# Squares of q and k ahead of weight splits and of the last scans, a softplus one split later, and unit-matrix products on TensorE around two norms

## What is computed

```python
xr, yr, qkv, z, beta_raw, alpha_raw = split(h @ w_in)          # layer 0, width 1024, 1024, 3072, 1024, ...
xr = dw_conv(xr, lru_cw, lru_cb)
q, k, v = split(silu(dw_conv(qkv, dn_cw)))
q = l2_normalize(q) * DN_DK ** -0.5;  k = l2_normalize(k)       # x * rsqrt(sum(x * x) + eps), per head of 128
g = -exp(dn_alog) * softplus(alpha_raw + dn_dtb)                # gates of the delta rule
lru = scan(a, b, forward) + scan(a, b, backward)                # then lru * gelu(yr)
...
x = x + g1 * mixer(rms_norm(x) * (1 + sc1) + sh1)
x = x + g2 * (square(relu(rms_norm(x) * (1 + sc2) + sh2) @ w1) @ w2)
```

## Time and profile before

| what | value |
|---|---|
| median of 3 runs | 1379.1 us (1378.88 to 1382.91) |
| profiled execution | 1384.1 us, its span 1382.3 us |
| mean granted TensorE clock | 0.992 of full speed |
| busy: PE, DVE, ACT, POOL | 1350.4 us (98%), 856.6 us (62%), 702.1 us (51%), 286.6 us (21%) |
| DMA | 170.88 MB, mean 124 GB/s |

### The profile page before, as it was taken

One profiled execution on the slowest core, in us unless ns is written; L12 is line 12 of the kernel. 1 busy time (PEld: TensorE's weight loads), 2 busy tenths in 40 slices (PEclk: granted clock), 3 DMA queues, 4 the chain that ended last, 5 costly groups with the idle time before them and its releaser, 6 DMA issues.

```text
span 1382.3 us, 28054 instructions
## 1 busy us (share of the span) xinstructions
PE 1350.4 (98%) x11226; PEld 1272.2 (92%) x11226; DVE 856.6 (62%) x1308; ACT 702.1 (51%) x1132; POOL 286.6 (21%) x296
## 2 busy tenths in 40 slices
PE   6999999999999999999999999999999999999998
PEld 3899999987799999899899999999998988999998
DVE  3754889884456565552577666666746666765563
ACT  4468888876545454521543311333225655673553
POOL 2000124231566777531100000000020000200002
PEclk8999999999999999999999999999999999999999
DMA  9623232321320010113355566565423311656562
GB/s 326 198 79 91 77 92 77 93 77 62 107 77 32 32 62 32 62 62 114 138 174 189 179 190 189 185 199 186 141 91 109 107 63 41 189 170 211 170 195 77
DMA packets 138030, 170.88 MB, mean 124 GB/s; under 512 B 10912, under 2 KB 121760, under 8 KB 137920
## 3 DMA queue, kind: packets, MB, share of 16 engines
q1 hardware_dynamic: 137312, 169.13, 38.8%
q0 software_dynamic: 608, 0.19, 0.1%
HBM read 168.25 MB, written 1.05 MB: 122 GB/s over the span
## 4 chain that ended last, share of the span: by engine, by line
PE 73%; ACT 1%; POOL 1%; DVE 1%; issue 1%; DVEq 0%; ACTq 0%; POOLq 0%
PE bank L2478 46%; PE bank L2485 7%; PE bank L2870 3%; PE bank L2858 3%; PE bank L2887 1%; PE bank L3109 1%; PE bank L2812 1%; PE bank L3132 1%; PE bank L2734 1%; PE bank L2836 1%; PE bank L2404 1%; PE bank L2847 1%; PE bank L2799 1%; PE bank L2824 1%; PE bank L2757 1%
## 5 line engine op out<-in xcount | busy, mean ns | idle before, releaser
L1619 DVE TENSOR_TENSOR w_lo<-raw,w_hi 128x1024 fp32r<-128x1024 f32 x216 | 270.0, 1251 | 320.4 <-ACT w_hi L906 319.8
L906 ACT ACTIVATE w_hi<-raw 128x1024 fp32r<-128x1024 f32 x216 | 227.7, 1055 | 382.8 <-PE bank L2478 380.0
L2478 PE MATMUL bank<-h_hi,w_hi 128*128 128x256 f32 x1472 | 302.2, 284 | 9.6 <-DVE w_lo L1619 4.1
L2478 PE MATMUL bank<-h_hi,w_lo 128*128 128x256 f32 x1472 | 295.6, 279 | 0.0
L2478 PE MATMUL bank<-h_lo,w_hi 128*128 128x256 f32 x1472 | 290.2, 280 | 0.0
L2478 PEld LDWEIGHTS bank<-h_hi,w_hi 128*128 128x128 f32 x1472 | 227.5, 189 | 20.3 <-issue 14.8
L2478 PEld LDWEIGHTS bank<-h_hi,w_lo 128*128 128x128 f32 x1472 | 227.1, 189 | 0.0
L2478 PEld LDWEIGHTS bank<-h_lo,w_hi 128*128 128x128 f32 x1472 | 224.3, 190 | 0.4 <-DVE h_lo L1865 0.4
L2478 PE MATMUL bank<-hid_hi,w_hi 128*128 128x256 f32 x768 | 173.2, 280 | 0.0
L2478 PE MATMUL bank<-hid_hi,w_lo 128*128 128x256 f32 x768 | 172.2, 278 | 0.0
L2478 PE MATMUL bank<-hid_lo,w_hi 128*128 128x256 f32 x768 | 172.1, 278 | 0.0
(11 more groups left out here) (349 smaller groups left out, 2474.9 us busy)
## 6 DMA issues: line engine op xcount, KB each, us to landing
raw<-in_mlp_w SPq DMA_DIRECT2D x128, 512.0 KB, 3.6
late_w<-in_w_mod SPq DMA_DIRECT2D x56, 512.0 KB, 4.4
raw<-in_even_w_in SPq DMA_DIRECT2D x48, 512.0 KB, 3.8
raw<-in_w_mod SPq DMA_DIRECT2D x24, 512.0 KB, 4.3
first_w<-in_w_mod SPq DMA_DIRECT2D x16, 512.0 KB, 11.1
raw<-in_even_w_out SPq DMA_DIRECT2D x16, 512.0 KB, 3.6
raw<-in_attn_w_qkv SPq DMA_DIRECT2D x16, 512.0 KB, 3.6
raw<-in_attn_w_o SPq DMA_DIRECT2D x8, 512.0 KB, 3.4
```

Of the source, the lines that this page charges most:

```text
L906: act.activation(stored(w_hi, j, four), raw[:, j % RAW], ACT.Copy).then_inc(hi_ready, 1)
L1619: dve.tensor_tensor(stored(w_lo, j, four), raw[:, j % RAW], stored(w_hi, j, four).bitcast(F32), ALU.subtract).then_inc(split_done, 1)
L2478: return pe.matmul(bank[2 * pair + t][:, c - n0:c - n0 + CTX], w_[:, k, t * P:(t + 1) * P], x_[:, c:c + CTX], start=(kk == 0 and first and ...
```

## The change

Four edits in the order of queues; nothing is computed differently. (1) In body 8, the first of z, the squares of group 1 stand first, then the split of u+2, the scaling of group 0, and only then the last output of the LRU. (2) In body 9 the squares of group 5 and the scaling of group 4 stand ahead of the split of u+2. (3) The softplus in body 2 moves from slot 1 to slot 2, behind the split of u+3 and the first evacuation. (4) TensorE multiplies the unit matrix after the sums of `mlp0` and `mix1` (five products with 256 columns of constants, two transposes of the unit matrix) and before the last unit of the first body of `up00`, `down00` and `down01` (four transposes each; the condition is `ready and late`). The results go to a PSUM bank that nobody reads.

```diff
@@ -142,6 +142,7 @@
 FIRST_PAIRS = ((0, 0), (1, 0), (0, 1), (1, 1))
 HALF = KT // 2
 WARM = 4
+NORM_WARM = {"mlp0": 5, "mix1": 5}
 OUT_BEHIND = {5: (0, 1, 2, 3), 6: (4, 5)}
 SUMS_BEHIND = {row: g for g, row in enumerate((3, 6, 10, 13, 17, 20, 24, 27))}
 BY_POOL = 18
@@ -1797,13 +1798,17 @@
             def body_beside(b, s, it):
 
                 u = 2 * s["upp"] * it + s["unit"]
-                if b == LRU_TILES:
-                    lru_output(b - 1)
+                if b < LRU_TILES:
                     split_lo(u + 2, 2)
                     beside(b, 0)
+                elif b == LRU_TILES:
+                    l2_squares(1)
+                    split_lo(u + 2, 2)
+                    l2_scaled(0)
+                    lru_output(b - 1)
                 else:
+                    beside(b, 0)
                     split_lo(u + 2, 2)
-                    beside(b, 0)
                 beside(b, 1)
                 split_lo(u + 3, 3)
                 evac(s, it, 0)
@@ -2033,7 +2038,7 @@
                                            gate_bias[:, 0, :].unsqueeze(1).to_broadcast([P, NT, 16]), ALU.add))
                     dve.scalar_tensor_tensor(out=sp_a[:, 0:64], in0=sp_x[:, 0:64], scalar=-1.0, in1=sp_x[:, 0:64], op0=ALU.mult,
                                              op1=ALU.max).then_inc(s_gate, 1)
-                if b == 2 and w == 1:
+                if b == 2 and w == 2:
                     dve.wait_ge(s_gate, 4)
                     softplus(0, 64)
                     dve.scalar_tensor_tensor(out=g_log[:, :, :], in0=sp_x[:, 0:64].rearrange("p (n c) -> p n c", c=16),
@@ -2042,7 +2047,7 @@
                 if b == LRU_TILES - 1 and w == 3:
                     dve.wait_ge(s_lps, LRU_TILES)
                     l2_squares(0)
-                if b >= LRU_TILES:
+                if b >= LRU_TILES and (b, w) != (LRU_TILES, 0):
                     g = 4 * (b - LRU_TILES) + w
                     if g < 7:
                         l2_squares(g + 1)
@@ -2549,6 +2554,9 @@
                 n, per_body = s["bodies"] - ends, 2 * s["upp"]
                 if ready or late:
                     for j in range(first, per_body):
+                        if ready and late and j == per_body - 1:
+                            for i in range(4):
+                                pe.transpose(bank[X1][:, 0:P], C("ident"), C("ident"))
                         unit(s, 0, j, hi, lo, n0, ready, low)
                         if late:
                             late_beside(s["unit"] - MLP0 + j)
@@ -2589,6 +2597,10 @@
                     pe.wait_ge(nrm["sq"], KT + 2 * (i - 1) + k - KT + 3)
                     mm = pe.matmul(bank[X0][:, 0:n], C("ones"), sq_of[name][:, k, 0:n], start=False, stop=(k == KT - 1))
                 mm.then_inc(nrm["ss"], 1)
+                for i in range(NORM_WARM.get(name, 0)):
+                    pe.matmul(bank[X1][:, 0:2 * P], C("ident"), cst[:, 0:2 * P], start=True, stop=True)
+                for i in range(2 if name in NORM_WARM else 0):
+                    pe.transpose(bank[X1][:, 0:P], C("ident"), C("ident"))
 
             def first_sum():
```

## The result

The changed kernel takes 1372.13 us (median of 5 runs, 1369.82 to 1374.19) against 1379.1 us (5 runs, 1377.39 to 1382.91): ratio 0.9946, 95% interval 0.9933 to 0.9958. Its profiled execution took 1374.19 us, its span 1372.4 us, at a mean granted clock of 0.995. The span fell by 9.9 us, the medians by 7.0. One run of one_up00 (4196.13 us) and one of z_warm (2246.12 us) are left out of the medians and ratios further down.

What follows compares the result with a forecast made beforehand. TensorE, busy 98% of the span, was the bound, with VectorE's loop pacing bodies 3 to 7. Terms -6.7 + 2.0 - 2.9 = -7.6 us gave a median of 1371.5 us, own range 1369.5 to 1373.5, chance 0.50.

Steps and rivals of the forecast that it cites:

- Squares in z: In z, TensorE's waits of 1.48 and 3.24 us for squares and 1.8 us of low clock go: -6.7 us.
- The new wait ahead of the split of u+2: In body 9 the scaling of group 4 awaits its roots, yet the split ends near 328 less 1.5, in time.
- rival (c): Waits in z move on instead of going: half of 6.7 lost gives 1374.9 us, all gives 1378.2; chance 0.18.
- Softplus: Moving it in body 2 makes VectorE reach body 3's LRU output later, so z starts later: +2.0 us.
- they lie beside the scans again: GpSimd's first silu products, at about 163, still overlap body 2's scans, which took 159.75 to 165.42 beside them.
- rival (b): The softplus costs nothing, as GpSimd's products miss the scans or VectorE catches up: -9.6 us, 1369.5; chance 0.13.
- The three or more waits for `w_lo` between 160 and 230 us: Sign in the new profile: TensorE's waits for `w_lo` become more in number there, three or more.
- I am wrong if z starts at the old time or earlier: Sign against the forecast, which had z itself starting 1.5 to 2.5 us later.
- Unit matrices at `mlp0` and behind: Clock -1.3, closer spacing in `up00` -2.9, transposes +0.44 there and +0.88 in `down00` and `down01`: -2.9 us.
- the 3.5 us of spacing: Loss in `up00` from matmuls 118 ns apart instead of 113.4 at full clock; 13/16 of it, 2.9, to be gained.
- it lasts until the four transposes at 782.84: The wide spacing of `up00` persists up to these transposes, directly behind which it is 113.4 ns again.
- Unit matrices at `mix1`: First eight rows at full clock, but q's third unit waits for VectorE's split: 0, bounds +0.2 and -0.7.

Runs made afterwards that it cites:

- one_up00: Changed kernel with one transpose instead of four before the fourth unit of `up00`, none in `down00` and `down01`: 1376.69 us, ratio 0.9976 to the kernel before.
- z_warm: Kernel before with the new z order and the unit-matrix products at both norms, no four transposes, softplus as before: 1374.43 us, ratio 0.9964.
- softplus_only: Kernel before with only the softplus of body 2 moved from slot 1 to slot 2: 1379.9 us, ratio 1.0001.
- silu_held: Kernel before with GpSimd's first silu held until the scans of body 2 are done, softplus not moved: 1378.07 us, ratio 0.9987.
- z_only: Kernel before with only the new order of bodies 8 and 9 in z: 1371.19 us, ratio 0.9941.
- z_four: Kernel before with the new z order and four transposes in `up00` only, no products at the norms, softplus as before: 1373.01 us, ratio 0.9959.
- no_warm: Changed kernel without the unit-matrix products behind the sums of `mlp0` and `mix1`, four transposes kept: 1373.41 us, ratio 0.9958 to the kernel before.

## Why the prediction came true, point by point

**Squares in z (-6.7 forecast, -7.34 measured): right.** The waits of 1.48 and 3.24 and the low clock's 1.8 went. The 0.6 that the sum lacked is spread over the stretches behind the two waits: from the sums of group 1 to those of group 2, 4 to 5, 5 to 6 and from group 7 to the delta rule each takes 0.15 to 0.3 us less, beside the wait and the low clock; in the stretch behind group 5 the rows stand 113.5 ns apart where they stood 117.8. I had named it as the bound of -7.2. Against softplus_only, which has the old order and the close spacing there (63.57), the gain is 6.8, as forecast; against silu_held, where the clock held (61.95), it is 5.2. The new wait ahead of the split of u+2 cost nothing, and rival (c) fell.

**Softplus (+2.0 forecast, 0.02 measured): wrong.** The step that failed is "they lie beside the scans again". `lru_scan(2)` did start later, by 1.67 us for 1.8 forecast. But I let GpSimd run its gate parts at the pace of the trace before (I put 2.4 us with the cast, the trace has 2.2) while VectorE was busy with instructions of two inputs. They took 6.1 us, the silus missed the scans, and the three instructions of the scan took 3.85 us for 5.67, 1.8 given back. That is rival (b), to which I gave 0.13. The three or more waits for `w_lo` between 160 and 230 us, which followed from this step, didn't come either; there was one. Of my own signs one speaks against me: "I am wrong if z starts at the old time or earlier". z starts at 289.29 us where it started at 289.42.

**Unit matrices at `mlp0` and behind (-2.9 forecast): right for the profiled execution, wrong for the kernel.** In the profile: -3.39 and +1.13, so -2.3. But the earlier trace rows showed one of two states. Against kernels with an untouched `up00` in the close state it is 88.78 - 88.9 = -0.1 and +0.9: the terms are a clock of -0.8 (88.12 against 88.9, forecast -1.3), transposes of +0.44 three times, and for spacing nothing. The step that failed is the 3.5 us of spacing, read as a constant from a single execution, and "it lasts until the four transposes at 782.84": it ended ahead of them, at `late_total` (5.66 us for the 48 matmuls between). The assumption that four transposes end it holds (72 of 72 places). In medians the transposes of `up00` are worth 3.0 to 4.8 us where the products are there, with intervals that overlap, where the profiles allow 3.0 (91.5 - 88.1 - 0.44), and nothing can be seen where they aren't (z_only 0.9941, z_four 0.9959). That they undo what the products bring more often is my reading of this and isn't shown. All of part (4) together measures 1.0003.

**Unit matrices at `mix1` (0 forecast): right**, with the wait of 1.2 us for `w_lo` at the third unit of q. It ran its first rows at full clock and gave the time back there: from the sums of `mix1` to the first sums for q and k it is 35.18 us where it was 35.34, and 34.8 to 35.5 in the other twelve.

**The total** was -7.6 forecast and -7.0 measured in medians, because two misses nearly cancel: +2.0 that didn't come, and -2.9 that is about nothing. That the number came so near is partly luck. The gain is z's alone. The profiled pair shows 9.9 because it set a wide `up00` against a close one.

What stays open: why the spacing changes, and whether it is wide more often behind the products. The traces only tell where it changes: at `late_total`, and inside a stream, in either direction, at a matmul that comes late. From 80 to 1030 us the fourteen traces have 51 such changes, each with a spacing of 120 ns or more at it, and as many late matmuls pass without a change. The share of wide executions is known from fourteen profiles only, since unprofiled runs show no spacing.

## What to carry to other kernels

Where a late instruction stands in a queue behind work that nothing waits for, and its own inputs are ready, moving it ahead can be worth its whole wait, and the low clock behind the wait besides, as in z here (7.3 us, for waits of 4.7 and a low clock of 1.8). A pace or a clock level that differs between two places of one trace may be a state of that execution: profile the same code two or three times (another kernel with that part untouched will do) before it goes into a sum as a constant. When a helper engine is moved in time, its durations must be taken anew beside its new neighbours.

## What was new about the hardware

- One stream of 256-column matmuls at granted clock 1.00 runs at 113.4 or at 117.8 ns each, for 70 us on end. Four transposes of 128 x 128 (0.44 us) ended the wide state each time (72 of 72), one (0.11 us) didn't, and behind the two products of `turned` it was wide in 25 of 112 places. Sixteen products with 32 columns of weights (`late_total`, 1.00 us) reversed the state in 70 of 70 places. The Trainium skill, in "TensorE: Matmul & The Clock Gate", section "Back-to-back issue gap", has a formula for an isolated matmul that gives 109 ns for 256 columns, and says that in a stream the weight loads count too. It tells of no second pace; both paces measured here lie above its 109 ns.
- GpSimd instructions of 0.20 to 0.32 us took 1.17 to 1.29 us beside VectorE's two-input instructions of 1.23 us, which weren't slowed; silus of 128 x 512 beside the same instructions made them 2.10 and 2.20 us. Evacuations from PSUM took 4.02 us for six with silus beside them (166.30 in body 2) and 4.03 without (152.08). The Trainium skill, in "SBUF — State Buffer", section "SBUF: two separate sides", says that GpSimd shares a pair of ports with VectorE's instructions that have two inputs in SBUF, and that whichever starts first holds it for its whole instruction. The durations here agree with that: beside VectorE's 1.23 us each small instruction of GpSimd lasts about as long and costs VectorE at most 0.04 us, while silus beside the same instructions add 0.9 to 1.0 us to VectorE's.
- After a wait of 2.9 us TensorE's clock was 0.50 for a while in some executions (1.71 us of full clock missing each time) and stayed at 1.00 in others, on the same piece of code: at `mlp0` it fell in z_four and not in no_warm.
